# A mixture of experts with gates and ups turned round: weights stationary, all rows of a group moving

## What is computed

```python
logits = h @ w_router + b_router                 # L x 32
top_val, top_idx = lax.top_k(logits, 4)
gates = softmax(top_val)
order = argsort(top_idx.reshape(-1))             # rows sorted by expert
tok = order // 4
hgu = lax.ragged_dot(h[tok], w_gate_up, group_sizes) + b_gate_up[e_sorted]
x_glu = minimum(hgu[..., ::2], 7)                # 1024 gates
x_lin = clip(hgu[..., 1::2], -7, 7)              # 1024 ups
act = x_glu * sigmoid(1.702 * x_glu) * (x_lin + 1)
out = lax.ragged_dot(act, w_down, group_sizes) + b_down[e_sorted]
out = out * gates.reshape(-1)[order][:, None]
moe = segment_sum(out, tok, num_segments=L)
```

## Time and profile before

| | before |
|---|---|
| median of three runs | 6021.41 us |
| the profiled execution | 6024.89 us |
| its span (first to last instruction) | 6023.7 us |
| instructions in it | 81192 |
| TensorE busy with matmuls | 5622.9 us, 93% |
| weight loads (beside the matmuls) | 4470.5 us, 74% |
| VectorE busy | 3616.1 us, 60% |
| ScalarE busy | 2339.5 us, 39% |
| GpSimd busy | 818.0 us, 14% |
| mean granted TensorE clock | 0.968 |
| experts stage, TensorE's first to last product | 3096 to 5938 us |

### The profile page before, as it was taken

The page is one execution under the profiler, slowest core; times in us unless marked ns, Lnnn a source line. Parts: engine busy times, 40 slices in busy tenths (PEclk is TensorE's granted clock), DMA queues, the critical chain, the costliest instruction groups (busy, mean ns, idle before and its releaser), DMA issues. The chain is left out here.

```text
span 6023.7 us, 81192 instructions
## 1 busy us (share of the span) xinstructions
PE 5622.9 (93%) x26367; PEld 4470.5 (74%) x26368; DVE 3616.1 (60%) x6999; ACT 2339.5 (39%) x4594; POOL 818.0 (14%) x612
## 2 busy tenths in 40 slices
PE   8999988987999999996979999999999999998994
PEld 7877766876777777765758788888887787876783
DVE  6766666222655566665755655655656655566767
ACT  3444412333333344443424334433444434344443
POOL 1110134322000000002521001000100001010102
PEclk9999999998999999998989999999999999999997
DMA  3333153445111101004325545544656535466666
GB/s 142 116 109 111 68 169 127 115 115 176 46 50 48 43 22 43 23 10 160 124 109 175 172 155 172 189 161 160 217 184 227 209 119 179 140 230 233 237 229 204
DMA packets 248601, 830.79 MB, mean 138 GB/s; under 512 B 21456, under 2 KB 154688, under 8 KB 207680
## 3 DMA queue, kind: packets, MB, share of 16 engines
q1 hardware_dynamic: 218240, 737.13, 34.6%
q0 software_dynamic: 27680, 85.41, 5.9%
q10 hardware_dynamic: 2336, 4.45, 0.2%
HBM read 689.78 MB, written 137.13 MB: 137 GB/s over the span
## 5 line engine op out<-in xcount | busy, mean ns | idle before, releaser
L2443 PE MATMUL ps<-e_wh,e_hTh 128*128 128x512 f32 x2496 | 1014.7, 407 | 14.7 <-PEq L2280 14.6
L2545 DVE TENSOR_TENSOR e_wl<-r_raw,e_wh 128x1024 fp32r<-128x1024 f32 x772 | 907.8, 1220 | 180.9 <-DVEq L2280 176.4
L2443 PE MATMUL ps<-e_wl,e_hTh 128*128 128x512 f32 x2496 | 992.3, 398 | 0.0
L2443 PE MATMUL ps<-e_wh,e_hTl 128*128 128x512 f32 x2496 | 991.4, 397 | 0.0
L2484 ACT CAST e_wh<-r_raw 128x1024 fp32r<-128x1024 f32 x772 | 769.5, 1050 | 21.2 <-ACTq L2280 16.1
L2443 PEld LDWEIGHTS ps<-e_wh,e_hTh 128*128 128x128 f32 x2496 | 472.7, 189 | 123.7 <-issue 20.1
L2521 ACT ACTIVATE e_gg<-e_gg 128x256 f32<-128x256 f32 x312 | 130.4, 418 | 1102.9 <-ACTq L2280 1102.9
L2443 PEld LDWEIGHTS ps<-e_wh,e_hTl 128*128 128x128 f32 x2496 | 472.2, 189 | 115.3
L2443 PEld LDWEIGHTS ps<-e_wl,e_hTh 128*128 128x128 f32 x2496 | 473.7, 190 | 103.2
L1688 PE MATMUL ps<-a_PT,a_V 128*128 128x512 f32 (+1 forms) x1088 | 548.9, 596 | 0.7 <-ACT a_oT L1744 0.7
L1757 DVE TENSOR_REDUCE a_sc<-ps 128x1 f32<-128x416 f32 (+1 forms) x640 | 364.7, 587 | 254.3 <-PE ps L1666 254.3
(11 more groups left out here) (353 smaller groups left out, 9238.0 us busy)
## 6 DMA issues: line engine op xcount, KB each, us to landing
r_raw<-in_wgu SPq DMA_DIRECT2D x130, 2048.0 KB
r_raw<-in_wdn SPq DMA_DIRECT2D x64, 2048.0 KB
m_raw<-in_w SPq DMA_DIRECT2D x56, 1024.0 KB, 4.9
e_bg<-in_bgu SPq DMA_DIRECT2D x32, 1024.0 KB
qTd<-p_qt SPq DMA_DIRECT2D x32, 640.0 KB, 6.5
e_bd<-in_bdn SPq DMA_DIRECT2D x32, 512.0 KB, 11.0
kTd<-p_kt SPq DMA_DIRECT2D x32, 448.0 KB, 3.7
a_Q<-qTd SPq DMA_DIRECT2D x7, 2048.0 KB, 8.6
```

Of the source, the lines that this page charges most:

```text
L2443: t = pe.matmul(E.G[g][:, :], x[:, b, k, :], y[:, c % 2, k, :], start=(n == 0), stop=(n == 23))
L2545: return dve.tensor_tensor(lo, src, hi.bitcast(F32), ALU.subtract)
```

## The change

In chunks 0 to 3 the roles are exchanged. Each chunk has four banks: gates 0-127, ups 0-127, gates 128-255, ups 128-255 (`g = 2 * j + z`). For each bank and k, 128 columns of weights are stationary and all rows of the group move at once, `v = 128 * r` of them (128, 256, 384 or 512). The products then stand with the outcome's columns on partitions, rows along the free axis, which is how the down product needs them. The transposes `acts`, their two copies, and `E.act` go away.

The length of the moving operand is fixed in an instruction, so TensorE, ScalarE and VectorE get one version of the four chunks per number of blocks, chosen by a tree of compares (`by_blocks`): first r <= 2 or r > 2, then inside these. For v = 128 (`v <= BOTH`) the high and low halves of the rows move in one matmul of 256 columns, into two halves of the bank, and a second matmul of 128 columns multiplies by the low weights: 256 matmuls for four chunks. The other three versions have 384 matmuls each.

The bias is now one number per partition. It is loaded as 16 x 128 (8 KB), turned once per group on TensorE (`bias`, at k = 4 of chunk 5) and added with the clamp in one VectorE instruction; for v = 128 ScalarE copies the second half out with the bias and VectorE adds. The 1 of `x_lin + 1` is folded into the ups' bias. The clamp on the upper side is written before Silu, that on the lower side with the product (`max` with -6 after adding 1). Weight splits of the next chunks are woven into `pair`, quarter by quarter, so raw buffers are given back in the middle of a chunk and not at its start. All semaphores are renewed accordingly. The down product's code is the same but for the place of the waits for `E.aT_full`.

Cut to its core:

```diff
-def rows_bank(b, hf, bulk):
-    return (2 * b + hf) % 3 if bulk else b % 2 if hf else 2
+def rows_bank(b, hf):
+    return (2 * b + hf) % 3
+BOTH = 224
+def by_blocks(eng, r, program, blocks=(1, 2, 3, 4)):
+    if len(blocks) == 1:
+        program(128 * blocks[0])
+        return
+    n = len(blocks) // 2
+    with eng.If(r <= blocks[n - 1]):
+        by_blocks(eng, r, program, blocks[:n])
+    with eng.If(r > blocks[n - 1]):
+        by_blocks(eng, r, program, blocks[n:])
...
-    def acts(c, b):
-        take(pe, E.act_full[b])
-        take(pe, E.t_free[b % 2])
-        for k in range(2):
-            t = pe.transpose(E.T[b % 2][:, k * 128:(k + 1) * 128], E.act[:, b, k * 128:(k + 1) * 128], ident[:])
-        t.then_inc(E.t_full[b % 2], 1)
+    def gate_up(v):
+        for c, j, z in itertools.product(range(4), range(2), range(2)):
+            g = 2 * j + z
+            first = j == z == 0
+            take(pe, E.g_free[g])
...
+            for k in range(8):
+                if first and k % 2 == 0:
+                    take(pe, E.w_full)
+                wh, wl = E.wh[:, c % 2, k, f], E.wl[:, c % 2, k, f]
+                if v <= BOTH:
+                    t = pe.matmul(both, wh, E.hT[:, :, k, 0:v], start=(k == 0), stop=False)
+                else:
+                    t = pe.matmul(E.G[g][:, 0:v], wh, E.hT[:, 0, k, 0:v], start=(k == 0), stop=False)
+                if first and k == 0:
+                    t.then_inc(E.w_free, 1)
+                if v > BOTH:
+                    pe.matmul(E.G[g][:, 0:v], wh, E.hT[:, 1, k, 0:v], start=False, stop=False)
+                t = pe.matmul(E.G[g][:, 0:v], wl, E.hT[:, 0, k, 0:v], start=False, stop=(k == 7))
+            t.then_inc(E.g_full[g], 1)
...
-        for c in range(6):
+        by_blocks(pe, r, gate_up)
+        for c in (4, 5):
```

That was the choice of a version and TensorE's part; on VectorE (`pair`, here for more than one block, and `gate_up`, which ScalarE has in the same order):

```diff
+    def pair(c, j, v, n, quarters):
...
+            take(dve, E.g_full[2 * j])
+            dve.tensor_scalar(x, p[:, 0:v], bg, 7.0, ALU.add, ALU.min).then_inc(E.glu, 1)
+            take(dve, E.g_full[2 * j + 1])
+            link(dve.tensor_scalar(y, q[:, 0:v], bu, 8.0, ALU.add, ALU.min))
+        dve.sem_inc(E.g_free[2 * j], 1)
+        dve.sem_inc(E.g_free[2 * j + 1], 1)
+        lows(n, quarters[0])
+        take(dve, E.sig)
+        dve.scalar_tensor_tensor(out=y, in0=y, scalar=-6.0, in1=x, op0=ALU.max, op1=ALU.mult).then_inc(E.a_full, 1)
+        for i in quarters[1:]:
+            lows(n, i)
+        take(dve, E.a_hi)
+        t = low(E.aTl[:, 2 * c + j, 0:v], y, E.aTh[:, 2 * c + j, 0:v])
...
+    def gate_up(v):
+        for c in range(5):
+            if c:
+                pair(c - 1, 1, v, c + 1, (0, 1))
+            else:
+                lows(c + 1, 0)
+                lows(c + 1, 1)
+            if c < 4:
+                lows(c + 1, 2)
+                pair(c, 0, v, c + 1, (3,))
```

More of the change, by code:

```diff
@@ L2438, in product @@
                 take(pe, E.w_full)
-            between(pe, c, b, r, rn, acts, rows, k)
-            if k == 6 and c == 4:
-                take(pe, E.aT_full[b])
-            for x, y in ((xh, E.wh), (xh, E.wl), (xl, E.wh)):
-                t = pe.matmul(E.G[g][:, :], x[:, b, k, :], y[:, c % 2, k, :], start=(n == 0), stop=(n == 23))
+            if b == 0 and c == 4 and k in (0, 6, 7):
+                take(pe, E.aT_full)
+            between(pe, c, b, r, rn, bias, rows, k)
+            for x, y in ((E.aTh, E.wh), (E.aTh, E.wl), (E.aTl, E.wh)):
+                t = pe.matmul(E.G[g][:, :], x[:, k, b * 128:(b + 1) * 128], y[:, c % 2, k, :], start=(n == 0), stop=(n == 23))
                 if n == 0 and b == 0:
@@ L2511, in experts_act @@
                         scale(4, b)
-            if c:
-                high((c + 1) % 6, c, r, rn)
+            for i in range(4):
+                between(act, c, 0, r, rn, bias, rows, 2 * i)
+                if c == 5 or i >= 2:
+                    high((c + 1) % 6, i)
             for b in range(4):
@@ L2516, in experts_act @@
                     if b > 0:
[L2517 to L2521 removed]
+                        for k in (2, 6):
+                            between(act, c, b, r, rn, bias, rows, k)
                     if c == 5:
@@ L2560, in rows @@
             over(E.hx_free[b % 3])
-    def lows(n, c, r, rn):
-        for i in range(4):
-            if c >= 0:
-                between(dve, c, 0, r, rn, acts, rows, 2 * i)
-            take(dve, E.hi_full)
-            low(E.wl[:, n % 2, 2 * i:2 * i + 2, :].rearrange("p k n -> p (k n)"),
-                E.raw[:, n % 2, 2 * i:2 * i + 2, :].rearrange("p k n -> p (k n)"),
-                E.wh[:, n % 2, 2 * i:2 * i + 2, :].rearrange("p k n -> p (k n)")).then_inc(E.w_full, 1)
-        over(E.raw_free[n % 2])
@@ L2596, in experts_dve @@
     dve.reg_mov(ahead, first)
-    lows(0, -1, None, None)
+    dve.memset(E.one[:], 0.0).then_inc(E.dv, 1)
+    take(dve, E.dv)
+    for c in range(4):
+        dve.memset(E.one[:, 4 * c + 2:4 * c + 4], 1.0).then_inc(E.dv, 1)
+    take(dve, E.dv, 4)
+    for i in range(4):
+        lows(0, i)
+    bias()
     for b in range(4):
         with present(dve, first, b):
-            rows(b, 0, rows_bank(b, 0, True))
-            rows(b, 1, rows_bank(b, 1, True))
+            rows(b, 0)
+            rows(b, 1)
     with groups(E, dve) as q:
```

200 lines of the change are left out of this document (115 added, 85 removed).

## The result

| | before | after |
|---|---|---|
| median of 4 runs, us | 6022.44 (6018.91 to 6024.48) | 6429.65 (6427.46 to 6431.44) |
| ratio, 95% interval | 1 | 1.0677 (1.0658 to 1.0695) |
| profiled execution: span, us | 6023.7 | 6430.2 |
| mean granted clock of TensorE | 0.968 | 0.937 |

The change makes the kernel 407 us slower; 6290 was forecast, with a range of 5985 to 6440.

What follows compares the result with a forecast made beforehand. TensorE's matmul stream was taken as the bound in groups of two or more blocks. Terms -60 + 22 - 18 + 275 + 48 = +267 on 6024.9 us, less 3.5, gave 6288, rounded to 6290 us; range 5985 to 6440.

Steps and rivals of the forecast that it cites:

- the branch tree: TensorE's expert loop: code no longer kept, two of three far jumps per group each wait 4.3 us, +275 us (120 to 461).
- the clock: TensorE after an idle stop: seven matmuls at the slower pace, 1.5 us in each of 32 groups, +48 us (0 to 90).
- the one-block groups: Three single-block groups, bound by VectorE: shorter product and a smaller stop before the down product, -18 us.
- the high case: High end of the forecast: three far jumps per group at 4.8 us (461) less 56, giving 6426 us.
- Turning of outcomes (-60): TensorE's stream in groups of two or more blocks: 600 transposes at 0.10 us removed, -60 us.
- Gates and ups (+22): Gates and ups of 17 two-block groups: 384 matmuls of 256 columns at 0.120 us, 46.1 against 44.8 us, +22 us.
- Vector and scalar work (0): VectorE and ScalarE in groups of two or more blocks: their work is covered by TensorE's products, 0 us.
- bias (0): Bias loads: 31 broadcasts of 1 MB become loads of 8 KB; no group of two or more waits for DMA, 0 us.
- Rival "fetches are hidden or do not happen" (5965): Jumps in TensorE's queue: code kept or waits covered by matmuls issued ahead, only -56 us remains, 5965 us; chance 0.19.
- Rival "loads of weights become the bound" (6480): Gates and ups on TensorE: each matmul waits for its own load of 0.188 us, 6480 us without any fetch; chance 0.06.

Runs made afterwards that it cites:

- the form whose code is kept: The changed kernel with TensorE versions for two, three, four blocks and the down product run twice, VectorE and ScalarE versions for two and four: 5966.49 us.
- the runs with idle code: Never-executed matmuls in TensorE's loop: 100 or 420 in the kernel before, 6188.22 and 6059.57 us; 96 in the changed kernel with rolled-up code, 6142.64 us.
- two pairs of runs: VectorE's and ScalarE's three-block version added beside TensorE's versions for two, three, four blocks, 6075.69 to 6096.95 us; removed from the change, 6429.65 to 6418.72 us.
- 1602: The kernel before with 100 matmuls that are never executed added to TensorE's loop between chunks 3 and 4: 6188.22 us, ratio 1.0276.
- 1502: The kernel before with 50 matmuls that are never executed added to TensorE's loop between chunks 3 and 4: 6021.86 us, ratio 0.9998.
- that of 1758: The changed kernel with rolled-up gates, ups and down product, plus 96 never-executed matmuls before the down product: 6142.64 us, ratio 1.0182.
- a loop of 1726: The changed kernel with TensorE versions for two, three, four blocks run twice, VectorE and ScalarE versions for two and four, down product not rolled up: 6075.69 us.
- one of 2242: The kernel before with 420 matmuls that are never executed added to TensorE's loop between chunks 3 and 4: 6059.57 us, ratio 1.0063.

## Why the prediction was right, and where its sizes were off

The direction and the mechanism were right: TensorE's code no longer kept, stalls at the group's start and before the down product by the branch tree, and a lower clock behind them. 407 us were measured against 267 forecast, and a group of two blocks is 11.9 us longer where some 8 were forecast. That the result still lies in the range is in part luck: the branch tree, the clock and the one-block groups were all too small, 6430 is 10 us below the upper end of 6440, and the high case that was worked out gave only 6426. Term by term:

- **Turning of outcomes (-60).** Not measured by itself. In the form whose code is kept, a group of two blocks in an undisturbed row takes 67.7 us against 70.8; 16 transposes at 0.10 are 1.6 of these 3.1 us, and the gates' stream is 1.4. The two agree with the term within 0.1 us a group.
- **Gates and ups (+22).** Wrong in sign, inside its bounds. I took 0.120 us for 256 columns; they start 0.113 apart, the value of the load's floor and not of the line through wider matmuls. 384 x 0.113 = 43.4 us against 44.8: -24 over 17 groups. Three blocks: 66.4 against the 67.4 I took.
- **Groups of one block (-18; its own product, (2 + 3.6) x 3, is 17).** Wrong, for a reason I didn't foresee: 53.5 became 78.2 us, +74 for three. They have 12.7 us of stalls at start and middle, and a third one in the down product. The changed kernel's timelines there, of TensorE, ScalarE and VectorE:

```profile
4877.27 1.94 PE L2440 MATMUL ps<-ident,e_hx 128*128 128x128 f32 x8 [5.30 <-PEq L2280]
```

```profile
4872.67 0.72 ACT L2558 ACTIVATE e_Y<-e_Y,e_own 128x512 f32<-128x512 f32 x1 [5.14 <-ACTq L2280]
```

```profile
4867.89 0.69 DVE L2613 TENSOR_TENSOR e_hT<-ps,e_hT 128x512 fp32r<-128x512 f32 x1 [4.28 <-DVEq L2280]
...
4874.53 2.36 DVE L2613 TENSOR_TENSOR e_wl<-r_raw,e_wh 128x1024 fp32r<-128x1024 f32 x2 [1.88 <-DVEq L2280]
4876.81 0.17 DVE L2627 TENSOR_TENSOR e_bgT<-ps,e_one 128x16 f32<-128x16 f32 x1
```

The turning of the next rows needs the bank `T[2]`, which holds the turned bias until VectorE has read it (4876.81), and VectorE stands behind ScalarE's and its own late starts (5.14 and 4.28 us idle; fetches, as I read them by the packets of q14 in the same stretch). Here nothing covers these two engines; I priced VectorE's operations and left out its fetches, though rows 4 and 5 showed them. Even where the code is kept a group of one block takes 66.0 us, worked on as two.
- **The branch tree (+275).** Right in kind, too small. Start and middle together: two blocks 13.4 us, three 11.0, four 11.4, one 12.7, which is 399 us, less 20 for the same places before: about +380. Two inputs were off. A stalled branch takes TensorE 5.1 us here (3.9 to 5.5 on average in the runs with idle code) and not VectorE's 4.3; I had named its longer packets and left them out. And the number exposed: with two and three blocks all three jumps show. The matmuls issued ahead cover only part of each: in the middle, most stalled branches last 5.0 to 5.6 us with two blocks and 6.2 to 6.4 with three, while TensorE stands for 3.3 to 3.9 and 3.4 to 3.6. That leaves some 1.7 us hidden at 0.113 us a matmul and 2.8 at 0.173, and more at the group's end, at 0.233. I had let them hide one jump whole. The sum lies inside the ends I gave, 120 and 461.
- **Clock (+48).** Too small. TensorE's waits in the stage are 407.2 us in the change and 40.6 in the form that is kept, 366.6 of the 463 us between them. The other 97 are work that runs slower, and 26 more are hidden in them, since the kept form spends 8.6 us more on each one-block group (43.4 against 34.8 for the gates and ups). So some 120 us against the kept form. The clock's own rows agree: in the stage TensorE is busy for 276 us at a granted clock of 0.50 in the change, 25 in the kept form and 48 before; half of the differences is 125 us against the kept form and 114, 3.6 a group, against the kernel before, where I counted one stop of 1.5 and there are two. The end I gave was 90. The waits' growth (407.2 less 57.7), the clock's 114 and the streams' -60 and -24 make 380 of the 407 us; the other 27 are not assigned.
- **Vector and scalar work (0), bias (0).** For two blocks and more the first held nearly: a version more costs 10 to 20 us by two pairs of runs. For one block neither did: the bias costs no transfer, but it occupies a bank that TensorE asks for next.
- **Rival "fetches are hidden or do not happen" (5965).** It is what the kernel with the shorter code does: 5966. That the numbers agree so well is partly luck, since its terms erred in both directions: the gates' +22 is -24, the one-block groups' -18 is +37 in that form.
- **Rival "loads of weights become the bound" (6480).** Out: 0.113 us a matmul, not 0.188.
- **The rule on the length of code.** The Trainium skill (Runtime: NRT & Kernel Launch, section Instruction fetch mechanics) gives TensorE room for 2048 instructions, and a wait to a taken branch whose target is not in the current window of two pages, 256 instructions each; I took that for the whole 2048. Taken by its words the window would have made the loop of before, 1400, wait as well, and no packet of q8 comes in its 2620 us. The 2048 gave the right side for 3372. As a limit for a loop they are too many: 1602 rows plus loads (1714 with the semaphore waits, counted in the built program) are fetched again in each round, 1564 (1659) and 1502 (1614) are not.

What stays open: which pieces of code exactly are kept. 9 packets a round arrive with the loop of 1602, 2 with that of 1758. By the 256 instructions a block that the same section of the Trainium skill gives, the first is 6.3 blocks long by this count. Code fetched ahead beyond the loop's end, which pushes out the loop's first piece, would explain the early edge and the two packets, one before the loop's end and one inside the stalled branch, but no run tests it. Why the same 825 matmuls cost 6076 us with useful and 6143 with idle code stays open too; the two differ in the form of the down product, in a bank and in the place of the code. And the length is no measure for VectorE either: with its waits its loop has 382 instructions before, with packets in every round (226 over the span), and 398 in the short form, with 73 packets and none in the 2620 us.

## What to carry to other kernels

Code of a loop is a resource with an edge: here a TensorE loop of up to 1564 matmuls, loads and other rows runs without a fetch, and one of 1602 stalls in every round, even if the added part never runs. Beyond the edge the length alone does not tell the price: a loop of 1726 stalled in 14 of 31 turns, one of 2242 with a far jump in 7. A specialised version in a loop can be paid for by rounds that never use it (3 of 32 used it, 25 turns stalled): count the loop's instructions, waits included, before you write it, and get the specialisation's gain by rolling up what repeats (chunks that share a buffer; a buffer chosen by a counter in the moving operand). The sign is a queue of instruction packets that is quiet in the kernel before and busy in every round after, with the idle time of the sequencer behind the branches.

## What the runs showed that I had not expected

- 100 matmuls that are never executed cost 168 us (2.8%), 50 nothing (ratio 0.9998), and 420 only 39 us. 2 packets a round in place of 9 suggest that the far jump leaves most of the 420 unfetched.
- One stall a round can be a matter of a single piece of code: 96 idle matmuls in the short form cost 176 us with 2 packets of 16 KB in most rounds.
- A stall by code costs twice: of TensorE's 66 idle times over 1 us in the changed stage 62 are followed by a stretch at a granted clock of 0.50, in all some 120 us beside 367 us of waits, against the form whose code is kept.
- A form that is 6.8% slower became 1.0% faster than the kernel before without a change to its result: mainly the program's length on three engines changed. Besides, groups of one block are worked on as two, those of three as four on VectorE and ScalarE, and block 0 keeps one bank.
